# Splitting one layer's gate projection in two, by gate, in a hybrid decoder trunk

## The reference

```python
mod = (c_act @ w_ada[l] + b_ada[l])          # c_act = silu(c); w_ada[l] is 1024 x 6144
shift1, scale1, gate1, shift2, scale2, gate2 = jnp.split(mod, 6, axis=-1)
h = rmsnorm(x, norm1_g[l]) * (1.0 + scale1) + shift1
...
x = x + gate1 * (y_mix @ w_out[l])
h2 = rmsnorm(x, norm2_g[l]) * (1.0 + scale2) + shift2
x = x + gate2 * hier_moe(h2, ...)
```

## Time and profile before

| | us |
|---|---|
| median of 3 runs | 581.92 (581.85 to 581.98) |
| the profiled execution's own time | 583.74 |
| its span in the trace | 581.8 |
| PE busy | 548.2 (94%) |
| DVE busy | 278.4 (48%) |
| ACT busy | 224.3 (39%) |
| read from HBM | 188.12 MB, 325 GB/s over the span |

### The profile page before, as it was taken

One profiled execution on the slowest core, in us unless ns is written; L12 is line 12 of the kernel. 1 busy time (PEld: TensorE's weight loads), 2 busy tenths in 40 slices (PEclk: granted clock), 3 DMA queues, 4 the chain that ended last, 5 costly groups with the idle time before them and its releaser, 6 DMA issues.

```text
span 581.8 us, 8006 instructions
## 1 busy us (share of the span) xinstructions
PE 548.2 (94%) x3222; PEld 356.2 (61%) x3222; DVE 278.4 (48%) x475; ACT 224.3 (39%) x386; POOL 17.0 (3%) x74
## 2 busy tenths in 40 slices
PE   7899989999999999999978999999996999999996
PEld 6578939868666344443357897786674744444433
DVE  3629954993481022222358489479438202222243
ACT  2527445632346222221237264554314623222121
POOL 3105000000000000000000000000000000000000
PEclk9999999999989999999979999999997999999999
DMA  8999993972999999999997743499288379999961
GB/s 303 386 386 367 402 353 144 424 309 96 425 408 412 413 414 413 414 413 411 403 387 282 277 151 126 190 402 393 74 315 335 137 296 394 413 413 413 412 269 75
DMA packets 51759, 189.79 MB, mean 326 GB/s; under 512 B 4650, under 2 KB 4730, under 8 KB 44292
## 3 DMA queue, kind: packets, MB, share of 16 engines
q1 hardware_dynamic: 50496, 185.62, 81.8%
q0 software_dynamic: 896, 2.45, 1.2%
q10 hardware_dynamic: 324, 1.13, 0.6%
HBM read 188.12 MB, written 1.06 MB: 325 GB/s over the span
## 4 chain that ended last, share of the span: by engine, by line
PE 69%; DVE 17%; DMA 6%; ACT 3%; issue 2%; SPq 1%; DVEq 0%; ACTq 0%
PE ps L1559 18%; PE ps L1585 9%; PE ps L1462 7%; PE ps L1539 6%; PE ps L1354 6%; PE ps L1347 6%; DVE wlo L790 5%; PE ps L1248 5%; PE ps L1601 4%; DMA raw<-in_w_ada_dram 4%; DMA raw<-in_w_down_dram 2%; DVE work L952 2%; DVE cbc L1005 1%; DVE tokmaj L947 1%; SPq L325 1%
## 5 line engine op out<-in xcount | busy, mean ns | idle before, releaser
L790 DVE TENSOR_TENSOR wlo<-raw,whi 128x1024 fp32r<-128x1024 f32 x64 | 75.6, 1220 | 35.6 <-ACT whi L500 35.4
L500 ACT ACTIVATE whi<-raw 128x1024 fp32r<-128x1024 f32 x64 | 65.4, 1057 | 36.5 <-PE ps L1347 14.3
L1559 PE MATMUL ps<-raw,qkT 128*64 128x512 f32 x256 | 58.3, 597 | 1.6 <-ACT work L740 1.6
L1585 PE MATMUL ps<-raw,work 128*64 128x512 f32 x256 | 58.5, 598 | 1.1 <-DMA raw<-in_w_down_dram 1.1
L1559 PE MATMUL ps<-raw,cbc 128*64 128x512 f32 x256 | 57.6, 594 | 0.0
L1185 DVE SCALAR_TENSOR_TENSOR work<-ps,cw,work 128x256 f32<-128x256 f32 x16 | 10.9, 683 | 95.8 <-ACT work L734 95.8
L1171 DVE TENSOR_TENSOR v_sb<-ps,gates 128x512 f32<-128x512 f32 x32 | 22.1, 692 | 69.1 <-PE ps L1585 69.1
L1347 PE MATMUL ps<-act_hi,whi 128*128 128x256 f32 x192 | 54.9, 286 | 0.0
L1347 PE MATMUL ps<-act_hi,wlo 128*128 128x256 f32 x192 | 54.3, 283 | 0.0
L1347 PE MATMUL ps<-act_lo,whi 128*128 128x256 f32 x192 | 54.3, 283 | 0.0
L1248 PE MATMUL ps<-raw,c_rep 128*32 128x512 f32 x384 | 45.6, 605 | 4.0 <-DMA raw<-in_w_ada_dram 4.0
(11 more groups left out here) (239 smaller groups left out, 862.7 us busy)
## 6 DMA issues: line engine op xcount, KB each, us to landing
raw<-in_w_ada_dram SPq DMA_DIRECT2D x40, 1024.0 KB, 12.7
raw<-in_w_gate_dram SPq DMA_DIRECT2D x64, 512.0 KB, 8.3
raw<-in_w_up_dram SPq DMA_DIRECT2D x64, 512.0 KB, 9.8
raw<-in_w_down_dram SPq DMA_DIRECT2D x32, 1024.0 KB, 11.3
raw<-in_w_in_dram SPq DMA_DIRECT2D x23, 1024.0 KB, 14.3
raw<-in_w_ada_dram SPq DMA_DIRECT2D x16, 512.0 KB, 11.4
raw<-in_w_out_dram SPq DMA_DIRECT2D x8, 1024.0 KB, 7.0
gates<-gate_line POOLq DMA_DIRECT2D x2, 1024.0 KB, 5.1
```

The source lines that it names most:

```text
L500: act.activation(whi[:, slot(n), :], raw[:, r, (i % 2) * 1024:(i % 2 + 1) * 1024], ACT.Copy).then_inc(hi_done, 1)
L790: dve.tensor_tensor(wlo[:, slot(n), :], raw[:, ring_slot[("w", l, i // 2)], (i % 2) * 1024:(i % 2 + 1) * 1024], whi[:, slot(n), :].bitcast ...
L1559: ins = pe.matmul(ps[i * SLOTS:(i + 1) * SLOTS, 0, :], hg[p // 2 % 2][:, k, c0:c0 + SLOTS], ws[i][:, :, kk, :], start=(k == 0), stop=(k == ...
L1585: ins = pe.matmul(ps[i * SLOTS:(i + 1) * SLOTS, 2 + n, :], hidT[:, p % 2, kk, i * SLOTS:(i + 1) * SLOTS], ws[i][:, c0:c0 + 512], start=(kk ...
```

## The change

Layer 1's chunk "G" becomes two chunks of 4 units each: "G1" (gate1) and "G2" (gate2). A unit holds two rows of w_ada for one gate, again 1 MB, and is multiplied with 8 matmuls of 256 columns. G1 takes the place of "G" on PE: 2 units before the transposes of q and k, 2 after. G2 is multiplied in the second norm and router of layer 1: 2 units before the transposes (L1296), 2 after the logits (L1511). In the stream G2 comes behind M. The gate row is added, written, read back and broadcast once for each gate, over 256 columns of four strips. `gate_row("G2")` stands on VectorE in front of the calculation of `over`, and VectorE waits for the last broadcast ahead of the first expert. Layer 0 is not changed.

```diff
-            chunks += [("G", l), ("M", l)] + ([("A", l + 1)] if l + 1 < L else [])
+            chunks += [("G", l), ("M", l), ("A", l + 1)] if l + 1 < L else [("G1", l), ("M", l), ("G2", l)]
...
-        chunk_units = [4 if kind in ("A0", "A1") else KD for kind, _ in chunks]
+        chunk_units = [4 if kind in ("A0", "A1", "G1", "G2") else KD for kind, _ in chunks]
...
-            stream += [("a", chunk_of[("G", l)], k) for k in range(KD)]
+            g, late = chunk_of[("G" if l + 1 < L else "G1", l)], chunk_of[("A", l + 1) if l + 1 < L else ("G2", l)]
+            stream += [("a", g, k) for k in range(chunk_units[g])]
             stream += [("w", l, u) for u in range(12, 16)]
             stream += [("a", chunk_of[("M", l)], k) for k in range(KD)]
-            if l + 1 < L:
-                stream += [("a", chunk_of[("A", l + 1)], k) for k in range(KD)]
+            stream += [("a", late, k) for k in range(chunk_units[late])]
...
+                    if which in ("G1", "G2"):
+                        c0 = (2 if which == "G1" else 5) * D
+                        src = ada_v[layer, :, 2 * i:2 * i + 2, c0:c0 + D]
+                        dst = dst.rearrange("p (j n) -> p j n", j=2)
...
+            for g, kind in enumerate(("G1", "G2")):
+                pool.wait_ge(mod_sum, steps_before[chunk_of[(kind, L - 1)]])
+                c0 = (3 * g + 2) * D
+                pool.dma_start(mod_rows[0:97:32, 0:256],
+                               b_ada[L - 1, c0:c0 + D].rearrange("(h n) -> h n", h=4)).then_inc(gate_bias, 16)
+                pool.wait_ge(gate_row_ready, L + g)
+                line = gate_line[L - 1, 2 * g:2 * g + 2].rearrange("r n -> (r n)")
+                pool.dma_start(line.rearrange("(h n) -> h n", h=4), mod_rows[0:97:32, 0:256]).then_inc(gate_out, 16)
+                pool.wait_ge(gate_out, 16 * (L + g))
+                if g == 0:
+                    pool.wait_ge(res_ready, T * (L - 1))
+                pool.dma_start(gates[:, g, :], line.partition_broadcast(P)).then_inc(gate_full, 16)
...
                 if l + 1 < L:
                     modulation("A", l + 1)
+                else:
+                    gate_row("G2", l)
                 dve.wait_ge(count_done, l + 1)
...
+                if l + 1 == L:
+                    dve.wait_ge(gate_full, 16 * (L + 1))
...
+                    if kind in ("G1", "G2"):
+                        for j in range(2):
+                            for i in range(4):
+                                c0 = j * D + 256 * i
+                                ins = pe.matmul(ps[32 * i:32 * i + 32, 6, 0:256], c_rep[:, 2 * k + j, :],
+                                                raw[:, ring_slot[unit], c0:c0 + 256],
+                                                start=(k == 0 and j == 0), stop=(k == 3 and j == 1),
+                                                skip_group_check=True)
+                        ins.then_inc(ada_used, 1)
+                        continue
...
-                ada_acc("G", l, range(0, 4))
+                gate_kind = "G" if l + 1 < L else "G1"
+                half_units = chunk_units[chunk_of[(gate_kind, l)]] // 2
+                ada_acc(gate_kind, l, range(0, half_units))
                 pe.wait_ge(rope_done, T * (l + 1))
                 qk_transposes(0)
                 qk_transposes(1)
-                ada_acc("G", l, range(4, 8))
+                ada_acc(gate_kind, l, range(half_units, 2 * half_units))
...
                 if l + 1 < L:
                     ada_acc("A", l + 1, range(0, 4))
+                else:
+                    ada_acc("G2", l, range(0, 2))
                 transposes(m, (4, 5, 0, 1))
...
                 if l + 1 < L:
                     ada_acc("A", l + 1, range(6, 8))
+                else:
+                    ada_acc("G2", l, range(2, 4))
                 pe.wait_ge(asg_ready, l + 1)
```

More of the change, by code:

```diff
@@ L267, in trunk @@
         for l in range(L):
-            chunks += [("G", l), ("M", l)] + ([("A", l + 1)] if l + 1 < L else [])
+            chunks += [("G", l), ("M", l), ("A", l + 1)] if l + 1 < L else [("G1", l), ("M", l), ("G2", l)]
         chunk_of = {q: i for i, q in enumerate(chunks)}
-        steps_before = [sum(1 for kind, _ in chunks[:i] if kind != "G") for i in range(len(chunks))]
-        chunk_units = [4 if kind in ("A0", "A1") else KD for kind, _ in chunks]
+        steps_before = [sum(1 for kind, _ in chunks[:i] if kind[0] != "G") for i in range(len(chunks))]
+        gates_before = [sum(1 for kind, _ in chunks[:i] if kind[0] == "G") for i in range(len(chunks))]
+        chunk_units = [4 if kind in ("A0", "A1", "G1", "G2") else KD for kind, _ in chunks]
         units_before = [sum(chunk_units[:i]) for i in range(len(chunks) + 1)]
@@ L328, in load @@
                         return
-                    if which == "G":
+                    if which in ("G1", "G2"):
+                        c0 = (2 if which == "G1" else 5) * D
+                        src = ada_v[layer, :, 2 * i:2 * i + 2, c0:c0 + D]
+                        dst = dst.rearrange("p (j n) -> p j n", j=2)
+                    elif which == "G":
                         src = row.rearrange("p (g n) -> p g n", g=2)[:, :, 2 * D:3 * D]
@@ L448, in _ @@
                              ).then_inc(rw_ready, 1)
-            for l in range(L):
+            for l in range(L - 1):
                 pool.wait_ge(mod_sum, steps_before[chunk_of[("G", l)]])
@@ L879, in modulation, with gate_row @@
                                          ).then_inc(mod_ready, 1)
-            def gate_row(l):
-                q = chunk_of[("G", l)]
+            def gate_row(kind, l):
+                q = chunk_of[(kind, l)]
+                width = 512 if kind == "G" else 256
                 dve.wait_ge(ada_used, units_before[q + 1])
-                dve.wait_ge(gate_bias, 32 * (l + 1))
-                dve.tensor_tensor(mod_rows[:, :], ps[:, 6, :], mod_rows[:, :], ALU.add).then_inc(gate_row_ready, 1)
+                dve.wait_ge(gate_bias, 32 * (L - 1) + 16 * (gates_before[q] - L + 2) if kind != "G" else 32 * (l + 1))
+                dve.tensor_tensor(mod_rows[:, 0:width], ps[:, 6, 0:width], mod_rows[:, 0:width], ALU.add
+                                  ).then_inc(gate_row_ready, 1)
             def activation_parts(l, banks):
@@ L986, in heads_out @@
                         .to_broadcast([P, T, 4, HD]), ALU.mult).then_inc(yatt_raw, 1)
-                gate_row(l)
+                gate_row("G" if l + 1 < L else "G1", l)
                 softmax_max(0)
@@ L1239, in ada_acc @@
                     pe.wait_ge(mod_evac, steps_before[q])
-                    before_q = sum(1 for name, _ in chunks[:q] if name == "G")
-                    if before_q:
-                        pe.wait_ge(gate_row_ready, before_q)
+                    if gates_before[q]:
+                        pe.wait_ge(gate_row_ready, gates_before[q])
                 for k in ks:
```

## The result

| | before | after |
|---|---|---|
| median | 583.1 us (20 runs, 580.58 to 587.24) | 579.71 us (20 runs, 575.96 to 582.3) |
| ratio | | 0.9944, 95% interval 0.9927 to 0.9961 |
| the profiled execution's own time, its span | 583.74, 581.8 | 579.8, 578.0 |

The kernel is 3.3 us faster (2.3 to 4.3). The prediction said 4.8 us and 577.1, in 575.5 to 579.2; the measured 579.71 is outside. Part of that is the base: with 20 runs the kernel before has a median of 583.1, 1.2 above that of the three runs shown. Taken off those 581.92, the measured 3.3 would give 578.6, inside the range. The rest is the change itself, which brings a third less than forecast. Executions of one kernel spread over some 6 us, so a single profile's span says little; stretches inside it say much.

What follows compares the result with a forecast made beforehand. It saw layer 1's rotation held by a late transfer, its router by PE waits, and the experts by PE with transfers nearly level. Rotation 4.4 plus router 0.4 took 4.8 off 581.92: 577.1 us, range 575.5 to 579.2.

Steps and rivals of the forecast that it cites:

- the cover of the new wait: First expert of layer 1: gate2's broadcast, allowed 16 us, covered by the product 15 us after the row's addition; cost nothing.
- the router: Layer 1's norm and router: G2's matmuls fill PE's gaps, 0.4 us gained, bounds 1.2 lost to 2.6 gained.
- The rotation: Layer 1's rotation: G1 needs half the PE time and no transfer wait, so scores start 4.4 us earlier.
- the full clock: Rival: clock stays full in layer 1's router, 2.6 us gained there, 574.9 us in all; chance 0.08.
- The prefetch: Experts' first loads: G2's four units take 10.2 us of transfers, fitting a 10.8 us idle gap; costed at nothing.
- The rival of transfer-bound experts: Prefetch not through at the first `gate_up`, PE waits at pair 6's down units; 10.2 us uncovered gives 587.0; chance 0.05.

Runs made afterwards that it cites:

- e8: Kernel before with idle matmuls filling layer 1's norm and router, plus 128 never-executed PE instructions in the branch not taken: 581.2 us, ratio 0.9963.
- e5: Changed kernel with VectorE's broadcast wait moved to its first use, plus 128 never-executed PE instructions: 576.54 us, ratio 0.9891; again 576.12 us, 0.9876.
- e3: Kernel before with 16 idle matmuls at each of the two places in layer 1's norm and router where G2 goes: 583.44 us, ratio 1.0004.
- e4: Kernel before with 128 never-executed PE instructions in layer 1's untaken branch for overfull experts: 585.04 us, ratio 1.0036.
- e9: Changed kernel, wait still ahead of the first expert, plus 128 never-executed PE instructions: 578.05 us, ratio 0.9905.
- e2: Changed kernel with only 8 of G2's 32 matmuls done; loads, waits and gate row stay: 579.06 us, ratio 0.9931.
- e7: As e5, but loading 1.6 MB less of the up weights of layer 1's second expert pair: 577.54 us, ratio 0.9920.
- e6: Changed kernel with layer 1's first down units and all loads behind them held back until gate2's broadcast has landed: 580.45 us, one run.
- e10: Kernel before with 256 never-executed PE instructions in the same untaken branch as e4: 582.95 us, ratio 0.9998.

## Why the prediction was wrong

Two terms that the sum put at nothing failed: the cover of the new wait (1.7 us) and the place of PE's code (2.1 to 2.7 us), which it didn't have at all. A third, the router, was mis-sized the other way. That the total is off by only 1.5 us is luck: the router's surplus hid nearly half of what was missing.

**The rotation was right.** 4.4 us were worked out, 4.3 measured; G1's instruction 57 ns, measured 58; the wait for the transfer is gone, ACT's copies were in time. The 62 ns a matmul of the Trainium skill ("TensorE: Matmul & The Clock Gate", section "Wait — 56ns, not 53.3ns?"), which hold with hardware decode off, aren't seen here either; how decoding was set no run here shows. The chain of waits and PE's order of time were enough for it.

**The router was mis-sized.** 0.4 us were taken in bounds of -1.2 to 2.6; it measured 2.6 in the changed kernel's profiles, and 2.2 over e8's runs, in the kernel before. I leaned on layer 0's 0.91 as the clock that a filled stage gets. That was one execution. PE's work in layer 0's stage is the same in every kernel here, and the stage shows two lengths: 19.1 us at 0.91 in eight profiles, 17.6 at 1.00 in six, of which e5's is

```profile
154.34:171.98 17.64, 16.44 (x149) 10.15 (x148) 14.34 (x40) 10.81 (x17) 0.56 (x1) 1.00 1.02 412
```

At 0.91 the whole loss is in the gather (5.5 us in place of 4.0), as in e8. With G2 or e3's filling, layer 1's stage is at 1.00 in nine of ten profiles. So the full clock, given 0.08, was the likely case; what decides between the two is open. The Trainium skill's rule that gaps in TensorE's work bring the clock down ("TensorE: Matmul & The Clock Gate", section "HAM oscillation — how this bites in real kernels"), which stood beside that rival, pointed the right way.

**"I allow up to twice: 16 us ... it is covered" was the first step that failed.** It measured 14.4 from the row's addition (446.05) to the landing (460.47), within the allowance. But 16 was more than the 15 it was set against, and the 15 was the distance to the product before the change. The router's gain moves the product, and the row stands behind the router's chain of small steps: the distance became 13.4, what the product would have had without a wait. A cover measured in the old profile was spent by the gain that I was forecasting. The text also named today's 8 us as what would be covered, though those were measured with the transfers nearly idle (87 GB/s over 367 to 371 us, the broadcast's own start included), and I had just filled that time with four more units. Price: 1.1 us of lateness and 1.7 us of slow `gate_up` behind it in the profile, 1.7 us in the runs. The clock's part of that price wasn't in any sum.

**A term was missing: the code's place.** The change adds 128 instructions to PE's program. The kernel has a branch right ahead of the last scatters, and the sum said nothing of loading code. It costs 2.1 us in the kernel before (e4), 2.3 to 2.7 in the changed one (e9); the profiles' C shows 1.0 to 2.0 of it. No row of before shows it, since the program stood well; but its trace has the 0.72 of "issue" at the branch, which was the place to ask.

**The prefetch** was costed at nothing, by a margin of half a microsecond. In the changed kernel there is no wait for a down unit in one profile and 0.4 us in the other; e2, with the old length of the router, has 1.6. But e3 and e4 wait 0.4 with the loads in the old order, so whether the four units eat the slack isn't shown: only e2's single execution points to it. The runs don't show a mean cost (e7). The rival of transfer-bound experts, 10 us, is refuted: the longest wait for a down unit is 1.9 us, and that with the loads held back (e6).

**The sum as measured:** rotation -4.3, router -2.2, wait +1.7, code +2.3: -2.5 us, beside 3.3 (2.3 to 4.3) and 2.8 (1.3 to 4.3) measured. The router's term is taken over from e8, and each term that comes from runs is uncertain by a microsecond or more either way.

## What to carry to other kernels

A cover that is measured in the old profile shrinks by what the change gains ahead of it: work out each slack again in the new order, and time a small transfer with the load that will then run beside it. Put a wait at the first use of what it guards, not at the head of the stage. Ask of a stage's clock in several executions before taking one row as its level. Where a change adds instructions ahead of a branch, try a few paddings in a branch that isn't taken before believing a small difference; here that was worth as much as half of the best idea.

## What the hardware showed that I had not expected

- 128 instructions that are never executed cost 2.1 us, 256 cost nothing (e4, e10).
- Where PE stops in the last scatter, it goes on 1.3 to 1.6 us after a 16 KB instruction transfer has ended (six profiles).
- Layer 0's norm and router, the same work of PE throughout, take 19.1 us at a clock of 0.91 or 17.6 at 1.00, from one execution to the next.
- 1.8 us of idle matmuls at each of two places in the router are worth 2.2 us (e8), where the clock of the 19.4 us around them goes up from a mean of 0.74 to 1.00 (e3) or 0.91 (e8).
- PE's idle time of 1.18 + 0.47 us at the first expert, with an otherwise full stage around it, was followed by a clock of 0.68 over the next 5.35 us; with 0.82 us of idle there (e5) the same instructions took 3.65.
- A write of four rows of 1 KB had POOL waiting 4.58 us beside the experts' loads and 1.36 without them; the 512 KB broadcast behind it 8.6 and 4.0 (e6).
